# The down projection of a feed-forward layer in two parts, with the sums of its norm formed ahead of the last chunk

## The reference, cut to what matters

```python
def swiglu_2(x, w1, w2):
    g, u = jnp.split(x @ w1, 2, axis=-1)
    return (jax.nn.silu(g) * u) @ w2
...
    for l in range(DEPTH_2):
        x = layer_norm(ALPHA * x + 0.5 * swiglu_2(x, ffn_w1[l, 0], ffn_w2[l, 0]),
                       ln_g[l, 0], ln_b[l, 0])
        mix = hybrid_mixer_2(x, w_in[l], b_merge[l], sc_w[l], rc_w[l], rc_b[l], rg_w[l],
                           rg_b[l], a_param[l], w_out_conv[l], w_out_rnn[l], w_o[l])
        x = layer_norm(ALPHA * x + mix, ln_g[l, 1], ln_b[l, 1])
        x = layer_norm(ALPHA * x + 0.5 * swiglu_2(x, ffn_w1[l, 1], ffn_w2[l, 1]),
                       ln_g[l, 2], ln_b[l, 2])
```

## Time and profile before

| | |
|---|---|
| median of 3 runs | 3602.77 us (3599.24 to 3606.78) |
| the profiled execution's own time | 3604.08 us |
| its span | 3602.3 us |
| TensorE busy | 3409.5 us, 95% |
| DVE, ACT, POOL busy | 1349.3, 1371.1, 1309.5 us (36 to 38%) |
| granted TensorE clock, mean | 0.977 of full speed |

### The profile page before, as it was taken

The page is one execution under the profiler, slowest core; times in us unless marked ns, Lnnn a source line. Parts: engine busy times, 40 slices in busy tenths (PEclk is TensorE's granted clock), DMA queues, the critical chain, the costliest instruction groups (busy, mean ns, idle before and its releaser), DMA issues.

```text
span 3602.3 us, 45142 instructions
## 1 busy us (share of the span) xinstructions
PE 3409.5 (95%) x16328; PEld 2816.4 (78%) x16328; DVE 1349.3 (37%) x1694; ACT 1371.1 (38%) x1818; POOL 1309.5 (36%) x547
## 2 busy tenths in 40 slices
PE   6998899899998999899899999999998989989997
PEld 4767799778887888788787888778887878878885
DVE  6763555532204220645315321242207452252214
ACT  3443344544324441325523443244323264234423
POOL 2232000134443444344443444334443434434443
PEclk8999999999999999999999999999999999999998
DMA  6331000123222222222222232222222222223222
GB/s 251 128 140 60 1 1 1 59 82 99 95 98 82 93 99 94 82 97 91 88 99 77 93 99 99 86 88 96 98 95 82 94 88 94 95 70 105 99 96 85
DMA packets 88878, 322.05 MB, mean 89 GB/s; under 512 B 9648, under 2 KB 10032, under 8 KB 88624
## 3 DMA queue, kind: packets, MB, share of 16 engines
q1 hardware_dynamic: 87424, 316.64, 26.2%
q10 hardware_dynamic: 1328, 3.67, 0.3%
HBM read 318.18 MB, written 2.10 MB: 89 GB/s over the span
## 4 chain that ended last, share of the span: by engine, by line
issue 60%; POOL 22%; PE 16%; ACT 1%; DVE 1%; POOLq 1%; DMA 0%; DVEq 0%; ACTq 0%; SPq 0%
POOL w_lo L420 22%; PE ps L443 4%; PE ps L444 4%; PE ps L448 4%; PE ps L790 1%; PE ps L863 1%; PE ps L867 1%; PE ps L864 1%; POOLq L419 0%; POOLq L99 0%; ACT w_hi L1017 0%; PE ps L890 0%; PE ps L888 0%; PE ps L889 0%; DVE X L1804 0%
## 5 line engine op out<-in xcount | busy, mean ns | idle before, releaser
L420 POOL TENSOR_TENSOR w_lo<-raw,w_hi 128x1024 fp32r<-128x1024 f32 x543 | 1309.3, 2412 | 2273.7 <-ACT w_hi L1017 2273.4
L1017 ACT ACTIVATE w_hi<-raw 128x1024 fp32r<-128x1024 f32 x543 | 575.0, 1060 | 1545.2 <-PE ps L448 946.6
L443 PE MATMUL ps<-acts,w_hi 128*128 128x512 f32 x2848 | 1111.8, 390 | 31.1 <-ACT tmp L1330 22.2
L444 PE MATMUL ps<-acts,w_hi 128*128 128x512 f32 x2848 | 1110.5, 390 | 0.0
L448 PE MATMUL ps<-acts,w_lo 128*128 128x512 f32 x2848 | 703.3, 389 | 0.0
L443 PEld LDWEIGHTS ps<-acts,w_hi 128*128 128x128 f32 x2848 | 536.3, 188 | 146.6 <-ACT w_hi L1017 32.2
L444 PEld LDWEIGHTS ps<-acts,w_hi 128*128 128x128 f32 x2848 | 536.3, 188 | 111.3
L448 PEld LDWEIGHTS ps<-acts,w_lo 128*128 128x128 f32 x2848 | 534.7, 188 | 110.9
L1823 DVE TENSOR_TENSOR tmp<-tmp,ps 128x512 f32<-128x512 f32 x110 | 75.7, 688 | 688.0 <-PE ps L448 628.1
L863 PE MATMUL ps<-acts,w_hi 128*128 (+1 forms) x760 | 295.6, 389 | 0.0
L864 PE MATMUL ps<-acts,w_hi 128*128 (+1 forms) x760 | 295.6, 389 | 0.0
(11 more groups left out here) (371 smaller groups left out, 3361.3 us busy)
## 6 DMA issues: line engine op xcount, KB each, us to landing
raw<-stream SPq DMA_DIRECT2D x543, 512.0 KB, 3.3
ada_behind<-ada SPq DMA_DIRECT2D x32, 512.0 KB, 3.6
ada_first<-ada SPq DMA_DIRECT2D x8, 1024.0 KB, 13.8
X<-x_in ACTq DMA_DIRECT2D x1, 2048.0 KB, 8.2
out<-X SPq DMA_DIRECT2D x8, 256.0 KB, 2.0
xin<-x_in ACTq DMA_DIRECT2D x2, 768.0 KB, 7.1
xin<-x_in SPq DMA_DIRECT2D x2, 768.0 KB, 9.2
rope_sb<-rope SPq DMA_DIRECT2D x1, 1280.0 KB, 9.2
```

Of the source, the lines that this page charges most:

```text
L420: nc.gpsimd.tensor_tensor(w_lo[:, slot, :, :], raw[:, slot % RAW, :, :], f32(w_hi[:, slot, :, :]), ALU.subtract).then_inc(s_lo, 1)
L443: mm(o, w_hi[:, s, k, :], xh, start=start, stop=False, skip_group_check=True)
L444: mm(o, w_hi[:, s, k, :], xl, start=False, stop=False, skip_group_check=True)
L1017: A(w_hi[:, s, :, :], raw[:, s % RAW, :, :], ACT.Copy).then_inc(s_hi, 1)
```

## The change

The down projection's chunks are cut in another way. Part one (`down_four`) is 11 chunks, each with 2 hidden tiles by the first 4 output tiles of `DOWN`; part two (`down_one`) is 11 chunks that go through the other 4 output tiles one after the other, 22 hidden tiles each. Products, chunks and weights are as many as before. The norm works on the first four output tiles as soon as part one is done, and on each of the others when its products are. The additions of squares and values no longer run a tile behind, and TensorE takes the products of the running sums with ones (`sums`) ahead of the last chunk (in the three other norms: right behind the last chunk, ahead of the last residual). ACT refills slots between the squares by the numbers in `LEAD`, and one slot after the last square. The change of `norm` and `normed` is common to all eight norms.

```diff
-TAIL = 3
+LEAD = (0, 0, 1, 0, 2, 3, 2, 2)
...
             def normed(seq, product, mean=True):
 
+                def sums():
+                    if mean:
+                        pe.wait_ge(s_sadd, n_s.up(KT - 2))
+                        mm(ps[seq[0]][:, :], ones[:, :], tmp[3][:, :], start=True, stop=False, skip_group_check=True)
+                    pe.wait_ge(s_qadd, n_q.up(KT - 2))
+                    mm(ps[seq[1]][:, :], ones[:, :], tmp[2][:, :], start=True, stop=False, skip_group_check=True)
+
                 for i in range(KT):
-                    product(i, seq[i])
+                    product(i, seq[i], sums)
                     if i:
                         pe.wait_ge(s_pre, n_pre.up())
...
+                down_four(0, True)
+                with rounds(pe, 2, (n_hi, 4), (n_lo, 4), (n_hid, 8)) as i:
+                    for j in range(4):
+                        down_four(i * 8 + 2 * (j + 1), False)
+                for c in range(9, FT // 2):
+                    down_four(2 * c, False)
...
+                def product(i, m, sums):
+                    if 4 <= i < KT - 1:
+                        for q in range(3 * (i - 4), min(3 * (i - 3), FT // 2)):
+                            down_one(q)
+                    elif i == KT - 1:
+                        down_one(FT // 2 - 2)
+                        sums()
+                        down_one(FT // 2 - 1)
...
-            def norm(seq, mean=True, keep=False, chunks_behind=0):
+            def norm(seq, mean=True, keep=False, ahead=(1,) * KT, chunks_behind=0):
...
                 for i, k in enumerate(seq):
-                    if not chunks_behind:
+                    for _ in range(ahead[i]):
                         done()
...
-            norm(DOWN, mean=False, chunks_behind=TAIL)
+            norm(DOWN, mean=False, ahead=LEAD, chunks_behind=1)
...
                     residual(k).then_inc(s_pre, 1)
                     pre.up()
+                    if i == KT - 1:
+                        break
+                    if mean and i:
+                        if i > 1:
+                            dve.wait_ge(s_sadd, sadd.now)
+                        dve.wait_ge(s_pre, pre.now)
+                        TT(tmp[3][:, :], X[:, seq[0], :] if i == 1 else tmp[3][:, :], X[:, k, :],
+                           ALU.add).then_inc(s_sadd, 1)
+                        sadd.up()
+                    dve.wait_ge(s_sqx, sqx.up())
                     if i:
-                        dve.wait_ge(s_sqx, sqx.up())
                         if i > 1:
                             dve.wait_ge(s_qadd, qadd.now)
-                        (CP(q, tmp[0][:, :]) if i == 1 else
-                         TT(q, q, tmp[(i - 1) % 2][:, :], ALU.add)).then_inc(s_qadd, 1)
+                        TT(q, tmp[0][:, :] if i == 1 else q, tmp[i % 2][:, :], ALU.add).then_inc(s_qadd, 1)
                         qadd.up()
```

More of the change, by code:

```diff
@@ L859, in down @@
                     pe.wait_ge(s_hi, n_hi.up())
[L860 to L864, removed]
+                    for i, (hh, hl) in enumerate(hidden_tiles):
+                        for j, m in enumerate(DOWN[:4]):
+                            mm(ps[m][:, :], w_hi[:, s, 4 * i + j, :], hh, start=(a and i == 0), stop=False,
+                               skip_group_check=True)
+                            mm(ps[m][:, :], w_hi[:, s, 4 * i + j, :], hl, start=False, stop=False,
+                               skip_group_check=True)
@@ L865, in down @@
                     pe.wait_ge(s_lo, n_lo.up())
-                    for m in seq:
-                        last = mm(ps[m][:, :], w_lo[:, s, m, :], hh, start=False, stop=False, skip_group_check=True)
+                    for i, (hh, _) in enumerate(hidden_tiles):
+                        for j, m in enumerate(DOWN[:4]):
+                            last = mm(ps[m][:, :], w_lo[:, s, 4 * i + j, :], hh, start=False, stop=False,
+                                      skip_group_check=True)
                     last.then_inc(s_done, 1)
-                seq = DOWN
@@ L871, in ffn @@
[L871 to L891, removed]
-                    if i < KT - 1:
-                        last.then_inc(s_out, 1)
-                    else:
-                        last.then_inc(s_done, TAIL)
+                down_four(0, True)
@@ new lines, in ffn, with down_one @@
+                with rounds(pe, 2, (n_hi, 4), (n_lo, 4), (n_hid, 8)) as i:
[3 more added lines that the diff above has]
+                    down_four(2 * c, False)
+                def down_one(q):
+                    s = slot[0] % SLOTS
+                    slot[0] += 1
+                    tiles = [(q, DOWN[4 + f // FT], f % FT) for f in range(TILES * q, TILES * (q + 1))]
+                    pe.wait_ge(s_hi, n_hi.up())
+                    for i, (_, m, k) in enumerate(tiles):
+                        mm(ps[m][:, :], w_hi[:, s, i, :], pair(8 + k)[0], start=(k == 0), stop=False,
+                           skip_group_check=True)
+                        mm(ps[m][:, :], w_hi[:, s, i, :], pair(8 + k)[1], start=False, stop=False,
+                           skip_group_check=True)
+                    pe.wait_ge(s_lo, n_lo.up())
+                    for i, (_, m, k) in enumerate(tiles):
+                        last = mm(ps[m][:, :], w_lo[:, s, i, :], pair(8 + k)[0], start=False, stop=(k == FT - 1),
+                                  skip_group_check=True)
+                        if k == FT - 1 and m != DOWN[-1]:
+                            last.then_inc(s_out, 1)
+                    last.then_inc(s_done, 1)
@@ L897, in ffn, with product @@
+                pe.wait_ge(s_prod, n_prod.now + 2)
+                def product(i, m, sums):
[6 more added lines that the diff above has]
+                        down_one(FT // 2 - 1)
+                seq = DOWN
                 normed(seq, product, mean)
             n_y = Tally()
-            def product(i, m):
+            def product(i, m, sums):
@@ L1281, in ffn @@
                         A(acts[:, bass.ds(i * 2 + (8 + j), 1), 0, :], tmp[1][:, :], ACT.Copy).then_inc(s_hh, 1)
-                with rounds(act, 4, *chunks(SLOTS)):
+                with rounds(act, 2, *chunks(SLOTS)):
                     for _ in range(SLOTS):
                         done()
-                for _ in range(FT - TAIL - 4 * SLOTS):
+                for _ in range(2 * SLOTS, FT // 2):
                     done()
@@ L1296, in _ @@
                 ffn()
-                norm(DOWN, chunks_behind=TAIL)
+                norm(DOWN, ahead=LEAD, chunks_behind=1)
                 for f in range(KT):
```

54 lines of the change are left out of this document (23 added, 31 removed).

## The result

The changed kernel takes 3640.15 us (median of 4 runs, 3639.11 to 3641.67), the kernel before 3603.64 us beside it. The ratio is 1.0103 with a 95% interval of 1.0085 to 1.0120: 1.0% slower, clear of the noise. The profiled execution has a span of 3639.9 us against 3602.3.

What follows compares the result with a forecast made beforehand. TensorE, busy for 95% of the span, was taken as the bound. Terms of 32+12+6.2+1.8−13−2.1 = +37 us on the profiled 3604.1 gave 3641, predicted as a median of 3640 us; range 3626 to 3650.

Steps and rivals of the forecast that it cites:

- Part 1, the stop: Between part one and part two, five places: TensorE waits for three residuals, 6.4 us each, +32 us.
- Part 2, the clock: Behind each of those five pauses: TensorE's granted clock is lower for a while, 2.4 us each, +12 us.
- Part 3, the mixers: Second block's two mixer norms: third residual late behind DVE additions that POOL holds, +3.1 us each, +6.2 us.
- Part 4, the first block's mixer: First block's mixer norm, once: TensorE's second chunk waits longer for the fourth residual, +1.8 us.
- Part 5, the norm's end: Five norm ends: opening 4.4 us earlier, net −2.6 each, −13 us; mixer norms −0.6 twice, −0.9 once.
- The sum: Whole kernel: all terms added, +37 us, predicted 3640 us, 1.0% slower; chance 0.72.
- B: Rival: the clock stays at its upper level through the five pauses, 3628 us; chance 0.08.
- C: Rival: further waits in part two, 2 to 3 us at each of five places, 3650 to 3655 us; chance 0.10.
- D: Rival: TensorE doesn't stop at the boundary of part one and part two, −7 us, 3596 us, faster; chance 0.05.

## Why the prediction was right

- **Part 1, the stop.** Predicted 6.4, measured 5.97 four times and 6.22 once (30.1 for 32). The chain was as written: first square 2.5 behind part one's end (2.61 predicted), third residual 5.16 behind it (5.44), TensorE 0.81 after its start. The difference is hand-overs of 0.03 to 0.04 us where 0.12 was taken. The run without the stop and the one with the early table show that the chain is what sets it.
- **Part 2, the clock.** Predicted 2.4 a place, measured 1.6 to 3.0, 12.8 in all for 12. Filling the stop without shortening it gave 9.7 by the profile and 11.2 by the median, so this is a price of its own.
- **Part 3, the mixers.** Predicted +3.1 a place, measured 3.02 (3.54 and 3.53 for 0.52). The second addition was held too (1.68, then 2.82), as the earlier trace rows had it; the reading of the Trainium skill ("SBUF — State Buffer", section "Who interferes with whom") by which DVE gets in first didn't come true. What the sum left out was the clock behind these two waits, +4.4. A wait of 3.5 us lowers it too; the sum had it only where a pause was as long as 4.8.
- **Part 4, the first block's mixer.** +1.8 − 0.9 predicted, +0.9 measured.
- **Part 5, the norm's end.** The opening 9.35 us behind the last residual, as predicted, and L1811 unheld at +7.28 (7.3 predicted). The two sums' products in the stream cost 1.7, for 1.82. The term took the layer norm's −2.6 for all five places; the first, without a mean, gave 2.63 − 0.86 = 1.8. The prediction names two causes, fewer products behind the last residual and fewer chunks for POOL. The runs show that the second gave nearly all of the gain, and that the first was a net loss behind the feed-forwards. The second block's mixer norms gave 0.8 each, for 0.6.
- **The sum** of +37 against +37.3 by the profile is better than its terms, and that is luck: the stops were 2 smaller, the mixers' clock 4.4 larger, and the clock behind the openings happened to be 2.4 kinder.
- **Rivals.** B (clock stays up) is refuted by the windows; C (further waits in part two) by the list of waits, which has nothing else ahead of L890 but 1.0 us in four pieces, in which the weight loads waited for ACT; D (no stop) by the trace. D's sum, 3596, is close to what the kernel without the stop measured, 3597.36.

What stays open is why the clock's price at one and the same place differs between profiles (the stops of the changed kernel cost 1.6 to 3.0, those of the run with the late sums 2.8 to 3.1 with the same 5.97 us of idle time); with the spread of the runs it keeps terms of 1 to 2 us from being confirmed by medians. Also open is whether the new order of additions (no longer a tile behind) helped or hurt behind the feed-forwards: no run changes it there.

## What to carry to other kernels

When one engine is the bound, read a wait that is written in its program in terms of what stands behind it: here the products of part two didn't need the residuals they stood behind, and leaving the waits out until the next place that needs them turned +37 us into −6. A stall of the bounding TensorE costs its length, and those of 3.5 to 6.2 us in this kernel another 1.6 to 3 us each at the lower clock; the five of 0.9 us left the clock at 1.00. When a group of changes comes together, take the parts singly: here the helpful one was the number of refills behind the last square, the one named in the title cost time behind the feed-forwards, and an order of additions that all norms share was wrong behind the mixers.

## What was not expected of the hardware

- Moving ACT's first square 1.5 us earlier brought only 0.57 us at four of five places, since a DVE addition with two SBUF inputs then fell under a POOL subtraction and took 1.69 us instead of 0.69.
- A DVE operation with one tensor in SBUF (TENSOR_SCALAR on X, L1823) took 2.44 us instead of 0.54 beside a POOL subtraction (1496.42 to 1499.27). The Trainium skill, "SBUF — State Buffer", section "Who interferes with whom", says that such an operation can enter a mode that uses both port pairs and then contends; this row agrees, and shows that counting inputs isn't enough to tell a safe DVE operation.
- Products that nobody uses, put in TensorE's idle time, made the kernel faster, in the stops by 9.7 to 11.2 us and ahead of the openings by 6.9 to 10.9.
